# Query silus between the exponentials, and the convolved rows split by row tile, in a two-layer decoder kernel

## The reference, cut to what matters

```
z = u @ w_in                                   # u: the normalised rows, 512 x 1024
q, f, inp, g, gate_b, gate_c, h_b = split(z)   # seven blocks of 512 columns
forget = lb + (1 - lb) * sigmoid(f)
o_a = hgrn2_chunkwise(silu(q), 1 - forget, inp, log(forget))   # exp of cumulative sums of the log
o_a = rms_norm(o_a, out_norm) * sigmoid(g)
o_b = gate_b * causal_depthwise_conv(gate_c * h_b, conv_w)     # width 3
h = h + concat([o_a, o_b]) @ w_out
```

## Time and profile before

| | |
|---|---|
| three runs | 1257.47, 1261.97, 1263.94 us; median 1261.97 |
| the profiled execution, its own time | 1258.92 us |
| its span in the profile | 1257.1 us |
| PE busy | 1162.2 us, 92% |
| DVE busy | 872.1 us, 69% |
| ACT busy | 735.6 us, 59% |
| granted clock of TensorE, mean | 0.965 |

### The profile page before, as it was taken

One profiled execution on the slowest core, in us unless ns is written; L12 is line 12 of the kernel. 1 busy time (PEld: TensorE's weight loads), 2 busy tenths in 40 slices (PEclk: granted clock), 3 DMA queues, 4 the chain that ended last, 5 costly groups with the idle time before them and its releaser, 6 DMA issues. The chain is left out here.

```text
span 1257.1 us, 16654 instructions
## 1 busy us (share of the span) xinstructions
PE 1162.2 (92%) x5728; PEld 935.3 (74%) x5728; DVE 872.1 (69%) x1116; ACT 735.6 (59%) x889; POOL 136.6 (11%) x98
## 2 busy tenths in 40 slices
PE   6989999896899999999897998996899999999986
PEld 4768887685788888888576785585678888888575
DVE  5633345726699999998556218925699999998654
ACT  5533220233688788878554328723577788778554
POOL 0000000001022122211100000000121222121100
PEclk9989999898899999999998898998799999999998
DMA  9312212132599999999471221122599999999431
GB/s 384 109 68 96 72 34 68 67 134 102 210 352 395 378 374 376 385 382 379 169 301 68 84 101 34 41 95 101 178 355 377 386 369 388 378 378 376 179 128 67
DMA packets 48435, 280.22 MB, mean 223 GB/s; under 512 B 9360, under 2 KB 9360, under 8 KB 19072
## 3 DMA queue, kind: packets, MB, share of 16 engines
q1 hardware_dynamic: 34256, 243.05, 51.0%
q0 software_dynamic: 14128, 36.48, 7.8%
HBM read 273.20 MB, written 23.07 MB: 236 GB/s over the span
## 5 line engine op out<-in xcount | busy, mean ns | idle before, releaser
L1463 DVE TENSOR_TENSOR wlo<-raw,whi 128x2048 fp32r<-128x2048 f32 x218 | 497.4, 2290 | 157.1 <-ACT whi L1008 146.5
L419 PE MATMUL psum<-whi,ahi 128*128 128x512 f32 (+1 forms) x1184 | 474.9, 401 | 28.5 <-DVE alo L1661 5.8
L1008 ACT ACTIVATE whi<-raw 128x2048 fp32r<-128x2048 f32 (+1 forms) x220 | 419.2, 1907 | 131.1 <-PE psum L419 127.4
L419 PE MATMUL psum<-whi,alo 128*128 128x512 f32 (+1 forms) x1184 | 463.6, 392 | 0.0
L419 PE MATMUL psum<-wlo,ahi 128*128 128x512 f32 (+1 forms) x1184 | 462.9, 391 | 0.0
L419 PEld LDWEIGHTS psum<-whi,ahi 128*128 128x128 f32 x1184 | 225.6, 191 | 77.9 <-issue 24.4
L419 PEld LDWEIGHTS psum<-whi,alo 128*128 128x128 f32 x1184 | 225.3, 190 | 47.7
L419 PEld LDWEIGHTS psum<-wlo,ahi 128*128 128x128 f32 x1184 | 226.2, 191 | 42.1
L1008 ACT ACTIVATE arena<-psum 128x512 f32<-128x512 f32 (+1 forms) x144 | 82.5, 585 | 136.5 <-PE psum L419 109.1
L1008 ACT ACTIVATE ahi<-psum 128x512 fp32r<-128x512 f32 x140 | 78.6, 594 | 100.5 <-PE psum L722 62.3
L419 PE MATMUL psum<-arena 128*128 128x512 f32 (+8 forms) x792 | 119.6, 325 | 10.4 <-DVE arena L1776 4.4
(11 more groups left out here) (170 smaller groups left out, 812.4 us busy)
## 6 DMA issues: line engine op xcount, KB each, us to landing
raw<-w_moe_dram SPq DMA_DIRECT2D x192, 1024.0 KB, 9.3
raw<-w_dense_dram SPq DMA_DIRECT2D x35, 1024.0 KB, 7.6
arena<-yscr POOLq DMA_DIRECT2D x8, 1024.0 KB, 8.0
vscr<-arena POOLq DMA_DIRECT2D x8, 512.0 KB, 2.9
arena<-gains_dram POOLq DMA_DIRECT2D x4, 512.0 KB, 3.4
arena<-w_proj_dram POOLq DMA_DIRECT2D x2, 1024.0 KB, 6.0
out_dram<-arena SPq DMA_DIRECT2D x3, 512.0 KB, 2.6
h<-x_dram SPq DMA_DIRECT2D x2, 512.0 KB, 6.2
```

Source lines behind the costliest of these rows:

```text
L419: return nc.tensor.matmul(o, l, r, start=start, stop=stop, **kw)
L1008: return nc.scalar.activation(o, i, ACT.Copy, scale=scale)
L1463: tt(wlo[:, b % SPL, :], raw[:, b % RAW, :], halves(whi[:, b % SPL, :]), ALU.subtract).then_inc(lo_ready, 1)
```

## The change

It has four parts. ACT does the silus of q's first three banks after the exponentials of tile 2 and before those of tile 3, and only the fourth silu after all of them. The convolution gets a third buffer (`AR_Y3`), so that feature tile 2 is convolved in the first pass of B; tile 3 reuses `yt` after `gate(0)`. The convolved rows are copied to `ahi` and split to `alo` by row tile, all four features of 128 rows at once, interleaved with the splits of the heads, and PE's tile q of out0 waits for `g_blo` at q + 1 in the place of 4. The gate product `rec(22)` moves behind the first two of these splits on DVE.

```
@@ out_before (PE)
-                    if i == 0 and q == 0 and k == BLK["out0"]:
-                        pe.wait_ge(g_blo, 4)
+                    if i == 0 and k == BLK["out0"]:
+                        pe.wait_ge(g_blo, q + 1)
@@ ACT, exponentials and silus
+            def query(tb):
+                group_done(act, BLK["q"], tb)
+                nc.scalar.activation(Q[:, tb, :], PS[tb][:, :], ACT.Silu).then_inc(g_silu, 1)
...
                 nc.scalar.activation(yt, PS[5][:, :], ACT.Exp).then_inc(g_esf, 1)
+                if tb == TB - 2:
+                    for q in range(TB - 1):
+                        query(q)
             nc.scalar.activation(dec, PS[6][:, 0:64], ACT.Exp).then_inc(g_dec, 1)
-            splits(6)
-            for tb in range(TB):
-                group_done(act, BLK["q"], tb)
-                nc.scalar.activation(Q[:, tb, :], PS[tb][:, :], ACT.Silu).then_inc(g_silu, 1)
+            query(TB - 1)
@@ ACT, copies before out0
-            for ft in range(4):
-                act.wait_ge(g_ob, ft + 1)
...
-                copy(ahi[:, 4 + ft, :], E[:, ft, :]).then_inc(g_bhi, 1)
+            def conv_hi(tb):
+                if tb == 0:
+                    act.wait_ge(g_ob, 4)
+                    act.wait_ge(w_used, first_chunk(BLK["out0"]))
+                copy(ahi[:, 4:8, tb * P:(tb + 1) * P], E[:, :, tb * P:(tb + 1) * P])\
+                    .then_inc(g_bhi, 1)
...
+            conv_hi(0)
+            conv_hi(1)
+            heads_hi(0)
+            conv_hi(2)
+            heads_hi(1)
+            conv_hi(3)
+            splits(17)
+            heads_hi(2)
+            heads_hi(3)
@@ DVE
+            def conv_out(ft):
+                return (yt, et, area(AR_Y3, 512), yt)[ft]
...
-                        if i == 0 and b == 2 and q >= 2:
-                            conv(q - 2)
+                        if i == 0 and b == 2 and q >= 1:
+                            conv(q - 1)
                         if i == 1 and b == 2:
                             gate(q)
-                            if q < 2:
-                                conv(q + 2)
-                        rec(b * 8 + i * 4 + q)
+                            if q == 0:
+                                conv(3)
+                        if b * 8 + i * 4 + q < 22:
+                            rec(b * 8 + i * 4 + q)
+            def conv_lo(tb):
+                dve.wait_ge(g_bhi, tb + 1)
+                dve.wait_ge(g_ob, 4)
+                w = (slice(None), slice(4, 8), slice(tb * P, (tb + 1) * P))
+                tt(alo[w], E[:, :, tb * P:(tb + 1) * P], halves(ahi[w]), ALU.subtract)\
                     .then_inc(g_blo, 1)
...
+            conv_lo(0)
+            conv_lo(1)
+            rec(22)
+            heads_lo(0)
+            conv_lo(2)
+            heads_lo(1)
+            conv_lo(3)
+            splits(17)
+            heads_lo(2)
+            heads_lo(3)
```

More of the change, by code:

```diff
@@ L95 @@
 AR_LBL, AR_LB = AR_Q, AR_ST
+AR_Y3 = 14848
 ARENA = 15360
@@ L1181, in _, with heads_hi @@
             out_root(3)
-            for ft in range(4):
-                act.wait_ge(g_ob, ft + 1)
-                if ft == 0:
+            def conv_hi(tb):
+                if tb == 0:
+                    act.wait_ge(g_ob, 4)
                     act.wait_ge(w_used, first_chunk(BLK["out0"]))
-                copy(ahi[:, 4 + ft, :], E[:, ft, :]).then_inc(g_bhi, 1)
-            splits(17)
-            for tb in range(TB):
+                copy(ahi[:, 4:8, tb * P:(tb + 1) * P], E[:, :, tb * P:(tb + 1) * P])\
+                    .then_inc(g_bhi, 1)
+            def heads_hi(tb):
                 act.wait_ge(g_oT, tb + 1)
@@ L1619, in rec @@
                     tt(G[:, t, :], K[:, t, :], G[:, t, :], ALU.mult).then_inc(g_oa, 1)
+            def conv_out(ft):
+                return (yt, et, area(AR_Y3, 512), yt)[ft]
             def conv(ft):
                 w = hc("convw")[:, ft * 3:ft * 3 + 3]
-                y = (yt, et)[ft % 2]
+                y = conv_out(ft)
                 if ft == 0:
@@ L1628, in conv @@
                     dve.wait_ge(g_ktail, TB)
-                if ft >= 2:
-                    dve.wait_ge(g_ob, ft - 1)
+                if ft == 3:
+                    dve.wait_ge(g_ob, 1)
                 link(ts(y, E[:, ft, :], w[:, 2:3], None, ALU.mult))
@@ L1637, in gate @@
                 group_done(dve, BLK["B"], ft)
-                tt(E[:, ft, :], PS[ft][:, :], (yt, et)[ft % 2], ALU.mult).then_inc(g_ob, 1)
+                tt(E[:, ft, :], PS[ft][:, :], conv_out(ft), ALU.mult).then_inc(g_ob, 1)
             splits(8)
@@ L1650, in _, with heads_lo @@
                             tt(E[:, q, :], PS[q][:, :], E[:, q, :], ALU.mult).then_inc(g_H, 1)
-                        if i == 0 and b == 2 and q >= 2:
-                            conv(q - 2)
+                        if i == 0 and b == 2 and q >= 1:
+                            conv(q - 1)
                         if i == 1 and b == 2:
                             gate(q)
-                            if q < 2:
-                                conv(q + 2)
-                        rec(b * 8 + i * 4 + q)
[L1658 to L1661, removed]
+                            if q == 0:
[7 more added lines that the diff above has]
+                tt(alo[w], E[:, :, tb * P:(tb + 1) * P], halves(ahi[w]), ALU.subtract)\
                     .then_inc(g_blo, 1)
-            splits(17)
-            for tb in range(TB):
+            def heads_lo(tb):
                 dve.wait_ge(g_mhi, tb + 1)
```

## The result

The changed kernel takes 1247.63 us (median of six runs, 1244.86 to 1250.45), against 1260.31 for the kernel before in the six runs beside it. The ratio is 0.9901, with a 95% interval of 0.9882 to 0.9920, so it is 1.0% faster; the forecast was 1247.7. A second measurement on another occasion gave 1247.08 against 1261.00, 0.9887 (0.9869 to 0.9904).

What follows compares the result with a forecast made beforehand. PE, busy 92% of the span, was taken as the bound; 3.93 + 2.61 + 4.37 + 1.86 = 12.8 us off 1258.92 or 1261.97 gave 1246.1 or 1249.2. The forecast was halfway, 1247.7 us, range 1242.5 to 1254.

Steps and rivals of the forecast that it cites:

- The first wait: Between blocks q and v, PE's 3.78 us pause for ACT's silu goes; PE reaches v 3.93 us earlier.
- its low clock: Matmuls behind each wait return from the 1.2 GHz level to the high rate: 2.61 us in v, 1.86 us in out0.
- The second wait: Between B and out0, PE's 5.81 us pause for DVE's split of convolved rows shrinks; PE resumes 4.37 us earlier.
- The forecast chain: Before out0: last gate 0.68, ACT copy 0.63, DVE split 0.69 plus short gaps; PE starts at 239.57, pause 1.44 us.
- rivals 2 and 4: Strided SBUF form slow or ACT's switches late (2: chance 0.08, 1250.6 to 1252.5 us); form far dearer, kernel slower (4: 0.03).
- The clock stayed high: Forecast before out0; rival 1 said the clock falls there all the same, gain 10.9, time 1249.6 us, chance 0.11.
- one row: Embedding gate in the old trace: eight transposes (1.04 us) and a pause of 2.04 us leave the clock high.
- The weight stream: Rival 3, expert stage: the experts' weight stream is the bound; gain 5.7 us, time 1254.8, chance 0.07.
- The sum: Gains between q and v and before out0, both waits and both low clocks: 12.8 us, 1.0%.
- The halfway choice between the bases: Whole kernel: 1247.7 us, halfway between 1246.1 (from the profiled execution's 1258.92) and 1249.2 (from the runs' median 1261.97).

Runs made afterwards that it cites:

- silu_only: The kernel before with only the silus of three tiles moved ahead of the last exponentials; 1252.70 us against 1259.54, ratio 0.9956.
- conv_only: The changed kernel with the silus put back behind all exponentials, so only the place before out0 is changed; 1253.83 us against 1259.54, ratio 0.9961.
- two_loads: The changed kernel plus two one-column activations of other table sets ahead of the three silus, so two more table loads; 1253.03 us against 1259.72, ratio 0.9944.
- rows_only: The kernel before with row-tile copies, splits and PE wait, but convolutions and gate product where they were; 1258.21 us against 1259.54, ratio 0.9994.
- order_only: The changed kernel's third buffer and late gate product, but feature-tile copies and splits, wait for all four, old silus; 1255.11 us against 1259.54, ratio 0.9973.
- heads_first: The changed kernel with out0's two weight chunks swapped, so convolved rows are needed only in its second pass; 1245.40 us against 1259.72, ratio 0.9882.
- wait_four: The changed kernel with PE's first tile of out0 waiting for all four splits of the convolved rows again; 1253.84 us against 1259.72, ratio 0.9954.

## Why the prediction was right, step by step

**The first wait** (3.93 us) and **its low clock** (2.61) were to give 6.54; the first piece gave 6.61. `silu_only` has it alone, 6.62, and `conv_only` doesn't have it. The last of the three silus ended at 73.15 by their row, 0.7 us ahead of v's first matmul, and the fourth silu at 78.07. This hiding of the loads has a limit, and `two_loads` shows it: with 3.0 us more on ACT, PE pauses.

**The second wait** (4.37) and **its low clock** (1.86) were to give 6.23; the second piece gave 6.34. The forecast chain left a pause of 1.44; measured was 1.39, since the last gate started 0.19 us behind the start of the transposes and not 0.26. The form 128x4x128 read from SBUF, not in the trace of before, took 0.62 to 0.63 on ACT and 0.68 to 0.69 on DVE, the value of its neighbours, so rivals 2 and 4 fell on their own term. The prediction costed one chain and didn't ask what each edit in it is worth: `rows_only` shows that the tiles give 0.7 us while the last gate is behind the gate product, and `order_only` that the order alone shortens the pause to 2.53 us, at which the clock still fell twice.

**The rivals.** The clock stayed high in all five traces with the pause of 1.39 us before out0. That it would was argued from one row, and for this place it came true. The row itself is weaker than it looked, so there was luck in it: the same pause of layer 0's embedding gate, with the same eight transposes ahead of it, ended low in 2 of the 13 traces, `conv_only` (2.05 us) and `heads_first` (1.98), while it stayed high at 2.11 and 2.12 us in others. In `conv_only`:

```profile
618.47 1.04 PE L487 MATMUL psum<-con,h 128*128 128x128 f32 x8
621.55 0.76 PE L420 MATMUL psum<-whi,ahi 128*128 128x512 f32 x1 [2.05 <-DVE alo L1527]
622.11 0.63 PE L420 MATMUL psum<-wlo,ahi 128*128 128x512 f32 x1
```

As a rule on pauses it didn't hold, see below.

The weight stream isn't the bound: from the first pause in the expert stage to the first one behind it lie 259.31 us before (345.46 to 604.77) and 259.34 after (332.94 to 592.28), with PE busy for 257.02 of 259.

**The size.** The sum, 12.8, was made against the profiled execution. By the two sets of medians the gain was 12.7 and 13.9 us. The halfway choice between the bases came within 0.1 us of the median, which is luck: spans of one kernel differ by 1.7 us between the two traces of the change, for what the clock and a DMA wait do later.

## What to carry to other kernels

Where one engine is busy for nearly all of the span (92% here), look for its pauses and for the low clock behind each, and count both: here one wait of 3.8 us removed and one of 5.8 shortened to 1.4 gave 12.9, a third of it the clock's. A wait split by tile is worth something only if what all tiles need (here the last gate) comes first on its engine, and an order made for it costs more than the old one if the wait stays whole (`rows_only`, `wait_four`). Shorten a pause until it is gone, since a pause of 1.34 us still cost the clock in `two_loads`.

## What the runs showed of the hardware that was not expected

The length of a pause doesn't say by itself what the clock does. Behind 1.34 and 1.35 us between q and v, with the cumulative sums ahead of it, it fell in both traces; behind 1.39 us before out0, with eight transposes ahead of it, it stayed high in all five. In the embedding gates the same pause ends either way, in the same kernel too. The one of 2.26 us in layer 1 left the clock high in 4 of 13 traces. The stage behind it, for PE alone, in the change:

```profile
1163.40:1168.00 4.60, 4.58 (x20) 1.00 0.19 70
```

The same in `silu_only`, at the 1.2 GHz level for most of it:

```profile
1166.80:1170.40 3.60, 3.60 (x9) 0.56 0.22 85
```

The first trace of `order_only` has it low there for eight matmuls, the second high.

What decides is left open; no run varied the work ahead of a pause with its length held. A fall costs 1.2 to 2.8 us (6 to 14 matmuls at 0.43 in the place of 0.23). In the rest of the kernel, where no run changed anything, the low matmuls numbered 34 to 56 and its length 987.0 to 992.7 us in thirteen traces. That spread of 5.7 us is nearly as much as either half of this change, and the reason to read a change of a few us in its own stage first and in the total afterwards.
